# Differential attention: projection rows one slot later, one at the head boundary, and the first key product of memory attention inside the last heads

## The reference, cut to what matters

```python
# A: differential attention, 8 heads of 2 x 64 (query, key) and 128 (value)
q = rope(rms_norm(q, q_g)); k = rope(rms_norm(k, k_g))
s = q @ k.T * 64 ** -0.5                 # two score maps a head, block-causal in chunks of 64
p = softmax(s); a = p[0] - lam * p[1]
o = rms_norm(a @ v, sub_g) * (1 - lambda_init)
# C: attention of the 512 rows to 256 memory rows, 4 heads of 256
k, v = split(rms_norm(mem, mem_g) @ w_kv); k = rms_norm(k, k_g); q = rms_norm(q, q_g)
o = softmax(q @ k.T * 256 ** -0.5) @ v
```

## Time and profile before

| | us |
|---|---|
| median of 3 runs (lowest to highest) | 2401.55 (2399.26 to 2403.48) |
| profiled execution | 2401.59 |
| its span, first to last instruction | 2400.0 |
| TensorE busy | 2254.4 (94%) |
| VectorE busy | 1589.4 (66%) |
| ScalarE busy | 1300.8 (54%) |
| GpSimd busy | 296.8 (12%) |
| differential attention, first projection to start of memory attention | 32.7 to 308.4 |
| granted TensorE clock, mean over the span | 0.963 |

### The profile page before, as it was taken

How to read it: one execution, slowest core, us unless ns; L and a number is a source line. 1 busy time by engine, 2 the same in 40 slices (tenths; PEclk the granted TensorE clock), 3 DMA queues, 4 the chain that set the end, 5 groups by cost and what they waited for, 6 DMA issues and landing times. The chain is left out here.

```text
span 2400.0 us, 30283 instructions
## 1 busy us (share of the span) xinstructions
PE 2254.4 (94%) x10196; PEld 1806.5 (75%) x10196; DVE 1589.4 (66%) x1790; ACT 1300.8 (54%) x1526; POOL 296.8 (12%) x391
## 2 busy tenths in 40 slices
PE   5888799799999999999979999999999999999997
PEld 4777577566566688888757888888888888888885
DVE  4676634454333433434559889889889888889884
ACT  5444434233232343323328777777777777777773
POOL 1232210200122100000111110110110110110110
PEclk8998889999899999999869999999999999999998
DMA  4111043221111233334459999999999999999992
GB/s 174 42 49 41 1 140 97 104 62 53 35 36 36 88 96 132 131 96 124 201 192 348 374 361 368 372 361 371 361 365 367 366 367 374 357 367 377 360 364 86
DMA packets 89013, 515.72 MB, mean 215 GB/s; under 512 B 15109, under 2 KB 16133, under 8 KB 38185
## 3 DMA queue, kind: packets, MB, share of 16 engines
q1 hardware_dynamic: 79736, 498.14, 55.9%
q0 software_dynamic: 9216, 16.81, 2.9%
HBM read 508.59 MB, written 23.33 MB: 222 GB/s over the span
## 5 line engine op out<-in xcount | busy, mean ns | idle before, releaser
L1961 DVE TENSOR_TENSOR moe_lo<-moe_raw,moe_hi 128x2048 fp32r<-128x2048 f32 x380 | 850.5, 2285 | 20.4 <-ACT moe_hi L1954 20.4
L1954 ACT ACTIVATE moe_hi<-moe_raw 128x2048 fp32r<-128x2048 f32 x380 | 728.4, 1919 | 171.6 <-PE bank L1972 162.2
L1970 PE MATMUL bank<-moe_hi,moe_XTh 128*128 128x512 f32 x1024 | 404.1, 395 | 0.0
L1971 PE MATMUL bank<-moe_lo,moe_XTh 128*128 128x512 f32 x1024 | 403.8, 394 | 0.0
L1972 PE MATMUL bank<-moe_hi,moe_XTl 128*128 128x512 f32 x1024 | 403.7, 394 | 0.0
L166 ACT ACTIVATE unit_hi<-unit_raw 128x1024 fp32r<-128x1024 f32 x116 | 122.5, 1059 | 282.0 <-DMA unit_raw<-in_w_units 266.9
L172 DVE TENSOR_TENSOR unit_lo<-unit_raw,unit_hi 128x1024 fp32r<-128x1024 f32 x116 | 141.7, 1225 | 180.5 <-ACT unit_hi L166 177.7
L1972 PEld LDWEIGHTS bank<-moe_hi,moe_XTl 128*128 128x128 f32 x1024 | 193.2, 189 | 44.5
L1971 PEld LDWEIGHTS bank<-moe_lo,moe_XTh 128*128 128x128 f32 x1024 | 193.3, 189 | 44.4
L1970 PEld LDWEIGHTS bank<-moe_hi,moe_XTh 128*128 128x128 f32 x1024 | 193.9, 189 | 40.3
L1970 PE MATMUL bank<-moe_hi,moe_aTh 128*128 128x512 f32 x512 | 200.8, 392 | 1.4 <-DVE moe_aTl L2082 1.4
(11 more groups left out here) (343 smaller groups left out, 3684.4 us busy)
## 6 DMA issues: line engine op xcount, KB each, us to landing
moe_raw<-in_w_moe SPq DMA_DIRECT2D x384, 1024.0 KB, 7.1
unit_raw<-in_w_units SPq DMA_DIRECT2D x116, 512.0 KB, 3.5
da_slab<-in_w_qkv SPq DMA_DIRECT2D x8, 1536.0 KB, 6.7
x_sb<-in_x SPq DMA_DIRECT2D x4, 512.0 KB, 5.1
yda_d<-y_daT SPq DMA_DIRECT2D x1, 2048.0 KB, 7.0
y_daT<-in_blocks_qk SPq DMA_DIRECT2D x1, 2048.0 KB, 8.1
y_daT<-yda_d SPq DMA_DIRECT2D x1, 2048.0 KB, 8.1
y_daT<-in_x SPq DMA_DIRECT2D x1, 2048.0 KB, 9.6
```

Of the source, the lines that this page charges most:

```text
L1954: nc.scalar.activation(HI[ring(n, pos)][:], RAW[pos][:], ACT.Copy).then_inc(s_hi, 1)
L1961: nc.vector.tensor_tensor(LO[pos][:], RAW[pos][:], HI[ring(n, pos)][:].bitcast(F32), ALU.subtract).then_inc(s_lo, 1)
L1970: nc.tensor.matmul(bank[:], xh[:, x], HI[ring][:, w], start=start and k == 0, stop=False)
L1971: nc.tensor.matmul(bank[:], xh[:, x], LO[pos][:, w], start=False, stop=False)
```

## The change

Differential attention: slots 0, 1 and 2 of head h multiply rows 1, 2 and 3 of head h+1. Row 0 of head h+2 is multiplied at the boundary in two halves of 4 steps of k, one ahead of `pv` of tile 3, one between `turn_qk(h+1)` and `scores(h+1, 0)`. Row 0 of head 1 comes ahead of `scores(0, 0)`. The orders of ScalarE, VectorE and GpSimd follow: `keep_proj(h+2, 0)` behind `exps(h+1, 0)`, `rope(h+2, 0)` behind the write of `y_daT`, `rotate(h+2, 0)` behind `o_rstd(h)`. Row 0 waits for its slab's remainder quarter by quarter.

Memory attention: the first key product is multiplied in heads 6 and 7 (`ca_keys`), into the two banks `pj`: unit 0 at the boundary of head 6, unit 1 in slot 0 of head 7, unit 2 in slots 1 and 2, unit 3 at the end. SP loads the four units of the first query product as the key units come free, and the first two are rounded and split in slots 1 and 3 of head 7. `stage_ca` begins with `group(0, "q")`.

```diff
@@ -289,10 +289,9 @@
-    projs = {0: [0], 1: [1], 2: [2, 3], 3: []}
...
@@ -320,23 +319,39 @@
...
                                  ).then_inc(s_w[par], 16)
+            for i in range(4):
+                sp.wait_ge(s_ku, i + 1)
+                refill(K, sp, 1, i)
...
         def _(pe):
-            def proj(n, par, i, first):
-                if not (first and i < 2):
+            def proj(n, par, i, ks=range(KT)):
+                if 0 in ks and not (isinstance(n, int) and n == 0 and i < 2):
                     pe.wait_ge(s_pjA, n * 4 + (i - 1))
-                if i == 0 and not first:
-                    pe.wait_ge(s_wl, n * 4 + 4)
-                for k in range(KT):
-                    if first and i == 0 and k % 2 == 0:
-                        pe.wait_ge(s_wl, k // 2 + 1)
+                for k in ks:
+                    if i == 0 and k % 2 == 0:
+                        pe.wait_ge(s_wl, n * 4 + (k // 2 + 1))
                     xh, xl = (x[:, k, i * P:(i + 1) * P] for x in (K.xnH, K.xnL))
...
                     mm = nc.tensor.matmul(bank, xl, wh, start=False, stop=(k == KT - 1))
-                mm.then_inc(s_proj, 1)
+                if KT - 1 in ks:
+                    mm.then_inc(s_proj, 1)
+
+            def ca_keys(u, t):
+
+                if u == 0:
+                    pe.wait_ge(s_pjA, NH * TT - 1 + t)
+                if t == 0:
+                    pe.wait_ge(K.s_wlo, u + 1)
+                for j in range(2):
+                    k, w, x = 2 * u + j, slice(j * 512, (j + 1) * 512), slice(t * P, (t + 1) * P)
+                    nc.tensor.matmul(pj[t][:], K.memH[:, k, x], K.whi[:, u, w], start=(k == 0), stop=False)
+                    nc.tensor.matmul(pj[t][:], K.memH[:, k, x], K.wlo[:, u, w], start=False, stop=False)
+                    mm = nc.tensor.matmul(pj[t][:], K.memL[:, k, x], K.whi[:, u, w], start=False, stop=(k == KT - 1))
+                if t == 1:
+                    mm.then_inc(s_ku, 1)
@@ -369,8 +384,14 @@
...
                         scores(h, par, i + 1)
-                    if more and projs[i]:
-                        proj(h + 1, 1 - par, projs[i][0], False)
+                    if i + 1 < TT:
+                        if more:
+                            proj(h + 1, 1 - par, i + 1)
+                        elif i == 0:
+                            ca_keys(1, 0)
+                            ca_keys(1, 1)
+                        else:
+                            ca_keys(2, i - 1)
                     if i:
@@ -380,12 +401,18 @@
...
                     mm.then_inc(s_aT, 1)
-                    if more:
-                        for t in projs[i][1:]:
-                            proj(h + 1, 1 - par, t, False)
+                if more2:
+                    proj(h + 2, par, 0, range(4))
+                else:
+                    ca_keys(0 if more else 3, 0)
                 pv(h, par, TT - 1)
...
                     turn_qk(h + 1)
+                if more2:
+                    proj(h + 2, par, 0, range(4, KT))
+                else:
+                    ca_keys(0 if more else 3, 1)
+                if more:
                     scores(h + 1, 1 - par, 0)
@@ -393,8 +420,9 @@
...
             for i in range(TT):
-                proj(0, 0, i, True)
+                proj(0, 0, i)
             turn_qk(0, True)
+            proj(1, 1, 0)
             scores(0, 0, 0)
@@ -439,8 +467,8 @@
...
                         exps(h, i + 1)
-                    if more and projs[i]:
-                        keep_proj(h + 1, 1 - par, projs[i][0])
+                    if more and i + 1 < TT:
+                        keep_proj(h + 1, 1 - par, i + 1)
                     act.wait_ge(s_aT, START + h * 4 + (i + 1))
@@ -450,14 +478,15 @@
...
                         unit_hi(K, act, 0, i)
-                    if more:
-                        for t in projs[i][1:]:
-                            keep_proj(h + 1, 1 - par, t)
+                    elif i % 2:
+                        act.wait_ge(s_ku, i // 2 + 1)
+                        unit_hi(K, act, 1, i // 2)
                 keep_o(h, TT - 1)
...
                     exps(h + 1, 0)
-
+                if more2:
+                    keep_proj(h + 2, par, 0)
@@ -468,6 +497,7 @@
...
             exps(0, 0)
+            keep_proj(1, 1, 0)
             heads(act, body, lambda: None)
@@ -491,16 +521,16 @@
...
             def body(h, par, more, more2):
-                for i in range(TT):
-                    if more and projs[i]:
-                        rotate(h + 1, projs[i][0])
-                    if more:
-                        for t in projs[i][1:]:
-                            rotate(h + 1, t)
+                if more:
+                    for i in range(1, TT):
+                        rotate(h + 1, i)
                 o_rstd(h)
+                if more2:
+                    rotate(h + 2, 0)
...
                 rotate(0, i)
+            rotate(1, 0)
             chain.restart()
@@ -558,12 +588,14 @@
...
                                                    ALU.add).then_inc(s_a, 1)
-                    if more:
-                        rope(h + 1, i)
+                    if more and i + 1 < TT:
+                        rope(h + 1, i + 1)
                     if more2:
...
                         unit_lo(K, dve, 0, i)
+                    elif i % 2:
+                        unit_lo(K, dve, 1, i // 2)
                 if more:
@@ -576,6 +608,8 @@
...
                                         ALU.mult).then_inc(s_yTe, 1)
+                if more2:
+                    rope(h + 2, 0)
@@ -588,6 +622,7 @@
...
             negmax(0, 0, False)
+            rope(1, 0)
             chain.restart()
@@ -624,12 +659,12 @@
...
             sp.dma_start(K.yda_d, K.y_daT[:]).then_inc(s_yd, 16)
-            for u in range(4, 28):
+            for u in range(8, 28):
                 group, i = (u - 4) // 4, u % 4
                 if i < 3:
-                    sp.wait_ge(s_use, 3 * group + i + 1)
+                    sp.wait_ge(s_use, 3 * (group - 1) + i + 1)
                 else:
-                    sp.wait_ge(s_row, NR * (group // 3) + (2, 6, 8)[group % 3])
+                    sp.wait_ge(s_row, NR * (group // 3) + (0, 4, 6)[group % 3])
                 refill(K, sp, u // 4, i)
@@ -715,7 +750,6 @@
...
-            group(0, "k")
             group(0, "q")
@@ -740,7 +774,8 @@
...
                 what, t = rows[r]
-                act.wait_ge(s_row, NR * n + r + 1)
+                if n or what != "k":
+                    act.wait_ge(s_row, NR * n + (r - 1))
                 if what == "v":
@@ -779,9 +814,9 @@
...
-            his(4, 7)
+            his(6, 8)
             keep_rows(0, "k")
-            his(7, 11)
+            his(8, 11)
             keep_rows(0, "q")
@@ -861,9 +896,9 @@
...
-            los(4, 7)
+            los(6, 8)
             norm_rows(0, 0, 2)
-            los(7, 11)
+            los(8, 11)
             norm_rows(0, 2, NQK)
```

More of the change, by code:

```diff
@@ L291, in stage_da @@
     (s_proj, s_pjA, s_pjD, s_ss, s_rope, s_qkT, s_qkTe, s_S, s_nm, s_exp, s_a, s_aT, s_aTe, s_pv, s_oss,
-     s_ors, s_on, s_yT, s_yTe, s_wh, s_wl, s_onr, s_kTe) = (K.sem("da_" + n) for n in (
+     s_ors, s_on, s_yT, s_yTe, s_wh, s_wl, s_onr, s_kTe, s_ku) = (K.sem("da_" + n) for n in (
          "proj", "proj_used_act", "proj_used_dve", "sumsq", "rotated", "qkT", "qT_kept", "scores",
-         "negmax", "exp", "a", "aT", "aT_kept", "pv", "o_sumsq", "o_rstd", "o_kept", "yT", "yT_kept", "slab_hi", "slab_lo", "o_scaled", "kT_kept"))
-    projs = {0: [0], 1: [1], 2: [2, 3], 3: []}
+         "negmax", "exp", "a", "aT", "aT_kept", "pv", "o_sumsq", "o_rstd", "o_kept", "yT", "yT_kept", "slab_hi", "slab_lo", "o_scaled", "kT_kept", "k_unit_used"))
     scale = DH ** -0.5
```

## The result

The changed kernel takes 2410.69 us (median of 8 runs, 2407.6 to 2412.93) against 2401.86 for the kernel before: ratio 1.0035, 95% interval 1.0022 to 1.0047. It is slower by 8.8 us; 2415 was forecast, with 2401 to 2427 as range. The profiled execution took 2407.76 us, near the lower end of its runs.

A forecast was written before the change was run, and what follows sets the result against it. In the heads neither TensorE nor VectorE is full, so the order of work decides. 13.5 (boundaries) + 4.5 (first head) - 10.9 (key product) + 0 (its pieces) + 5.9 (clock) = +13.0 on 2401.6, about 2415 us; range 2401 to 2427.

The forecast's parts named there:

- T(2) to T(3) stays 5.2 us: In each head, T(i) being the transpose of probability tile i: removing the projection row gains 0, leaving TensorE waiting 3-4 us.
- the first rival: Differential attention: TensorE paces every slot, so the boundary's 3.1 us of waits are won six times; 2377 us, chance 0.05.
- Boundary +2.45 at full clock: Between two heads, T(3) to T(0) grows from 11.95 to 14.4 us.
- The chain behind scores(0): In the boundary, from scores(0) through negmax(0), rope of row 0, negmax(1) and a(0) to T(0): 7.25 us.
- T(0) to T(1): First slot of a head: rope no longer waits for a late projection row; 6.2 instead of 6.4 us, -0.2.
- +13.5: Six boundaries with a row of head h+2, +2.25 us each; bounds +0.8 to +3 each.
- The clock +5.9: A clock fall near T(3) in each of seven heads, 2.0 us each, less 8.1 before; bounds -8.1 to +12.9.
- Ahead of the first head +4.5: Before scores(0, 0): row 0 of head 1 now stands there, taken as 5.7 us; first T(0) later by 2.8 to 6.6.
- The key product -10.9, its pieces 0: 48 matmuls leave memory attention's start, -10.9 us (other end -13.2); added inside heads 6 and 7, 0 (-2 to +4).
- the remainder of unit 0: Last head: VectorE's remainder of query unit 0 (1.2 us) stands before negmax(3), costing +0.9 us.
- the filled boundary: Rival: the filled boundary holds the clock, no falls, full clock into memory attention; -7.0, 2395 us, chance 0.10.
- as often as before: Rival: in the heads the clock falls as often as before, so no clock term; +7.1, 2409 us, chance 0.22.

The follow-up runs named there:

- tensor_only: Changed kernel with its TensorE order kept, but projection work of ScalarE, VectorE and GpSimd in the order of the kernel before: 2388.03 us, ratio 0.9954.
- fill_wait: Changed kernel plus 12 discarded matmuls between T(2) and slot 3's value product in heads 0 to 5: 2400.01 us, ratio 0.9994.
- keys_only: Kernel before plus only the first key product inside heads 6 and 7, without the new projection order: 2387.9 us, ratio 0.9941.
- row_in_wait: tensor_only with row 0 of head h+2 cut into TensorE's waits: behind T(2), ahead of T(3), ahead of scores(0): 2374.59 us, ratio 0.9892.
- keys_fill: keys_only plus 16 discarded matmuls in the three TensorE waits of each boundary 0 to 5: 2376.93 us, ratio 0.9906.

## Why the prediction was right, and where its sizes were not

- *T(2) to T(3) stays 5.2 us.* 5.13 to 5.15 in all six heads. The wait is 2.5 us (3 to 4 forecast). This excludes the first rival (2377 us): busier TensorE did not mean that TensorE sets the pace. `tensor_only` against the changed kernel shows it from the other side. The prediction cites the Trainium skill ("Perfetto Trace Analysis", section "Identifying the Most-Contended Engine") for that rival. The same section warns that for TensorE the busy share of matmuls tells little of how near its limit it is, and names the share of the weight loads among the better measures; by it the two engines are nearly level (PEld 22.68, DVE 22.21 of 30 us), so the section names no clear winner here.
- *Boundary +2.45 at full clock.* The step that was mis-sized. `fill_wait` shows 13.85 instead of 14.4. scores(0) came at 6.55, not 7.15, because I summed durations of matmuls whose ends overlap the next start: the value product lasts 1.05 us, and the transposes behind it start after 0.89. The chain behind scores(0), 7.25 forecast, took 7.33. T(0) to T(1) gained 0.4, not 0.2. Together 1.4 us a head instead of 2.25. What the prediction missed is the loop's turn, 0.5 us more in heads 1 and 3. With head 1 taken like head 3, six heads without a fall are an estimated 4 x 31.56 + 2 x 32.06 = 190.4 us, +9.5 over 180.9 where the sum had +13.5.
- *The clock +5.9.* A fall in each of seven heads, as forecast, but each cost more than the 2.0 of the sum: over six heads 204.6 - 190.4 = 14.2 us (2.4 each) against 8.1 before, +6.1; in head 6 about 1.8 more (T(3) to T(0) 11.82 against 10.06 in `keys_only`, which has no fall there). +7.9 in all. The Trainium skill ("TensorE: Matmul & The Clock Gate", section "HAM oscillation — how this bites in real kernels") tells of a loop with one long wait in each iteration and a fall in each. The seven heads agree with it, with no wait longer than 2.53 us in the first six (3.0 in head 6). The kernel before doesn't agree with it as the prediction words it: waits of up to 1.2 us recur in its every boundary, and the clock fell in three of six.
- *Ahead of the first head +4.5:* +4.6.
- *The key product -10.9, its pieces 0:* -11.7 in memory attention; in `keys_only` head 6 is 0.1 us longer and the last head as long as before. Within that zero the remainder of unit 0 cost 1.85 instead of 0.9, offset by the clock.

The two large errors had opposite signs (-4.0 and +2.0). The rest of the distance from 13.0 to 8.9 is the key product (0.8) and the last heads. That the time came within 4.3 us of the forecast owes something to this. Two rivals fall by their mechanism: the filled boundary did not hold the clock (2395 us), and the falls did not come as often as before (2409 us), but in every head. In its number the second of them was nearer to 2410.69 than the forecast was, so the time alone would not have decided between them.

## What to carry to other kernels

Before moving work from one slot to another, look at what ends last in both: the slot that gives it up gained nothing because another engine filled the same time, and the slot that took it paid. Moving one engine's work does not oblige the others to move theirs: the same matmuls with the old order on the other three engines were 22.7 us faster, part of it by shorter falls of the clock. A piece cut to the length of waits that exist was the best here (`row_in_wait`), and it kept the clock in the six heads. And a cost that hides beside a slack engine, like the loop's turn on VectorE, shows once that engine sets the pace.

## What the runs showed of the hardware

Discarded matmuls in TensorE's waits paid for themselves: `fill_wait` gained 10.7 us over the changed kernel (9.8 by the ratios) and `keys_fill` 11.0 over `keys_only` (8.4 by the ratios), of which the heads explain 7.7. Pauses far shorter than a low stretch were enough for a fall: none of TensorE's waits in heads 0 to 5 of the changed kernel was over 2.53 us, and each of the seven low stretches lasted 6.8 us. In `tensor_only` most lasted 3.4.

In the changed kernel the falls came at a steady distance: 120.7, 154.9, 189.0, 223.1 and 257.3 us, 34.1 apart. The heads are as long on average, but vary from 33.8 to 34.6 us; the falls were steadier than the work that they hit, and no head escaped. Why the distance is so even is not shown.
